# Gate half tiles of an mLSTM stage in four pieces between the products of a chunk, and the first gate tile back in the input projection

## What is computed

```python
def mlstm_chunk(carry, blk):                       # one block of L positions
    C, n, m = carry
    q, k, v, ig, lf = blk
    b = jnp.cumsum(lf, axis=-1)
    dmat = jnp.where(causal, b[..., :, None] - b[..., None, :] + ig[..., None, :], -jnp.inf)
    inter = b + m[..., None]
    m_row = jnp.maximum(inter, dmat.max(-1))
    s = jnp.einsum('bhtd,bhsd->bhts', q, k) * jnp.exp(dmat - m_row[..., None])
    w_prev = jnp.exp(inter - m_row)
    num = w_prev[..., None] * jnp.einsum('bhtd,bhde->bhte', q, C) + jnp.einsum('bhts,bhse->bhte', s, v)
    den = w_prev * jnp.einsum('bhtd,bhd->bht', q, n) + s.sum(-1)
    h = num / jnp.maximum(jnp.abs(den), jnp.exp(-m_row))[..., None]
    ...                                            # C, n and m for the next block

def mlstm_out(h, o, p):
    ...                                            # h is normalised per head
    h = h.reshape(Bsz, S, A_VW) * jax.nn.sigmoid(o.astype(F32))
    return h.astype(o.dtype) @ p['w_pa']
```

## Time and profile before

| | |
|---|---|
| median of 3 runs | 3401.12 us (3394.28 to 3404.74) |
| profiled execution, device time | 3390.82 us |
| its span, first to last instruction | 3389.2 us |
| TensorE busy | 3202.9 us, 95% of the span |
| DVE, ACT busy | 1357.8 us, 1071.0 us |
| mean granted TensorE clock | 0.967 |

### The profile page before, as it was taken

The page is one execution under the profiler, slowest core; times in us unless marked ns, Lnnn a source line. Parts: engine busy times, 40 slices in busy tenths (PEclk is TensorE's granted clock), DMA queues, the critical chain, the costliest instruction groups (busy, mean ns, idle before and its releaser), DMA issues.

```text
span 3389.2 us, 68441 instructions
## 1 busy us (share of the span) xinstructions
PE 3202.9 (95%) x27738; PEld 3007.9 (89%) x27738; DVE 1357.8 (40%) x1874; ACT 1071.0 (32%) x1585; POOL 133.6 (4%) x168
## 2 busy tenths in 40 slices
PE   8999999989998999999999999999899999999997
PEld 7999988867777989999999998988677789899996
DVE  3333345366333453333433334434653334533334
ACT  3222233244343323222232222332534433322223
POOL 0000000000330000000000000000013200000000
PEclk9999999799998999999999999988999989999999
DMA  5232221021552332222233222301035323223321
GB/s 134 87 90 83 82 73 49 7 59 55 204 221 56 87 93 69 87 86 85 60 101 92 86 82 61 95 23 47 23 116 221 147 75 100 62 87 88 88 86 55
DMA packets 443329, 296.56 MB, mean 88 GB/s; under 512 B 24327, under 2 KB 430571, under 8 KB 434985
## 3 DMA queue, kind: packets, MB, share of 16 engines
q1 hardware_dynamic: 430265, 217.05, 22.9%
q0 software_dynamic: 12928, 77.64, 6.1%
HBM read 286.44 MB, written 8.34 MB: 87 GB/s over the span
## 4 chain that ended last, share of the span: by engine, by line
PE 88%; DVE 5%; ACT 3%; issue 2%; DMA 0%; ACTq 0%; DVEq 0%; SPq 0%
PE ps L639 65%; PE ps L998 3%; PE ps L1013 2%; PE ps L747 2%; PE ps L1034 2%; PE ps L679 1%; PE ps L944 1%; DVE x_lo L1605 1%; PE ps L667 1%; PE ps L779 1%; PE ps L1016 1%; PE ps L935 1%; PE ps L922 1%; ACT prob L1418 1%; PE ps L1050 1%
## 5 line engine op out<-in xcount | busy, mean ns | idle before, releaser
L1553 DVE TENSOR_TENSOR w_lo<-w_raw,w_hi 128x1024 fp32r<-128x1024 f32 x436 | 533.5, 1225 | 1006.7 <-ACT w_hi L1198 1001.1
L639 PE MATMUL ps<-x_hi,w_hi 128*128 128x268 f32 x3904 | 814.1, 290 | 25.9 <-DVE x_lo L1605 17.6
L1198 ACT ACTIVATE w_hi<-w_raw 128x1024 fp32r<-128x1024 f32 x436 | 460.1, 1057 | 1170.6 <-PE ps L639 1158.7
L639 PE MATMUL ps<-x_lo,w_hi 128*128 128x268 f32 x3904 | 804.7, 288 | 0.0
L639 PE MATMUL ps<-x_hi,w_lo 128*128 128x268 f32 x3904 | 803.3, 287 | 0.0
L639 PEld LDWEIGHTS ps<-x_hi,w_hi 128*128 128x128 f32 x3904 | 612.9, 190 | 34.1 <-DVE x_lo L1605 24.5
L639 PEld LDWEIGHTS ps<-x_lo,w_hi 128*128 128x128 f32 x3904 | 615.4, 190 | 0.0
L639 PEld LDWEIGHTS ps<-x_hi,w_lo 128*128 128x128 f32 x3904 | 611.9, 189 | 0.0
L639 PE MATMUL ps<-h_hi,w_hi 128*128 128x268 f32 x1408 | 289.8, 288 | 5.0 <-issue 2.9
L639 PE MATMUL ps<-h_hi,w_lo 128*128 128x268 f32 x1408 | 290.9, 288 | 0.0
L639 PE MATMUL ps<-h_lo,w_hi 128*128 128x268 f32 x1408 | 289.4, 287 | 0.0
(11 more groups left out here) (376 smaller groups left out, 3914.1 us busy)
## 6 DMA issues: line engine op xcount, KB each, us to landing
w_raw<-in_ffn_up SPq DMA_DIRECT2D x180, 512.0 KB, 3.8
w_raw<-in_w_in SPq DMA_DIRECT2D x72, 512.0 KB, 3.9
w_raw<-in_ffn_down SPq DMA_DIRECT2D x64, 512.0 KB, 3.8
w_raw<-in_ffn_down SPq DMA_DIRECT2D x32, 384.0 KB, 3.4
w_raw<-in_w_o SPq DMA_DIRECT2D x16, 512.0 KB, 3.8
c_smp<-in_state_C SPq DMA_DIRECT2D x16, 256.0 KB, 3.0
out_new_C_sample<-c_smp SPq DMA_DIRECT2D x16, 256.0 KB, 2.4
w_raw<-in_w_pa SPq DMA_DIRECT2D x16, 256.0 KB, 2.8
```

The lines of the kernel that those rows point to most:

```text
L639: ins = mm(ps[0:m, 2 * p + half, 0:HT], w[:, s, off + t_ * m:off + t_ * m + m], x[part][:, k0 + t_, half * HT:(half + 1) * HT], start=firs ...
L1198: f(w_hi[:, s, :], w_raw[:, s, :], ACT.Copy).then_inc(hi_made, 1)
L1553: v.tensor_tensor(w_lo[:, s, :], w_raw[:, s, :], w_hi[:, s, :].bitcast(F32), ALU.subtract).then_inc(lo_made, 1)
```

## The change

The first gate tile (`B_QK` + 12) becomes the thirteenth tile of the input projection: a whole `product` on TensorE behind the loop, with `hi`, bias and `lo` of block `B_PAIR` + 0 behind it on ACT and DVE. Three tiles are left for the chunk stage, six half tiles: one whole behind `chunk_in(0)`, and one in each of the first five passes, cut into four pieces of 6 matmuls. The pieces stand ahead of `chunk_in(c + 1)`, inside it behind the mask, behind it, and behind line 807. The sixth pass has none. ACT reads each half tile where it did, behind the exponential of its pass. `lo` of `B_PAIR` + 1 to 3 stands behind sample steps 2, 4 and 6 instead of 1, 3, 5 and 7.

```diff
@@ TensorE, mlstm
-                pe.wait_ge(turned_read, l * 9 + 4)
-                gate_part(0, 0, 0, KT)
                 pe.wait_ge(conv_silu, l * 9 + 9)
...
-                def chunk_in(c):
+                def chunk_in(c, gate=None):
...
                     mm(ps[0:CH, 0, 0:HA * CH], ident_b[:, :], mask_b[:, :].unsqueeze(1).to_broadcast([CH, HA, CH]), start=False, stop=True).then_inc(ch_in, 1)
+                    if gate is not None:
+                        gate_part(*gate, 2, 4)
...
                 chunk_in(0)
-                gate_part(0, 1, 0, KT)
+                gate_part(1, 0, 0, KT)
                 for c in range(NCH):
...
                     chunk_we(c, 1)
                     if c + 1 < NCH:
-                        chunk_in(c + 1)
-                    gate_part(1 + c // 2, c % 2, 0, KT // 2)
+                        gate = 1 + (c + 1) // 2, (c + 1) % 2
+                        gate_part(*gate, 0, 2)
+                        chunk_in(c + 1, gate)
+                        gate_part(*gate, 4, 6)
...
-                    gate_part(1 + c // 2, c % 2, KT // 2, KT)
+                    if c + 1 < NCH:
+                        gate_part(*gate, 6, KT)
@@ TensorE, behind the loop of the input projection
+                pe.wait_ge(proj_read, l * PROJ + LINE_TILES)
+                ready(l, B_QK + 3 * HA)
+                product(2, B_QK + 3 * HA, KT, P, XX, True, True).then_inc(w_used, 1)
                 mlstm(l)
@@ ACT, in_projection
-                for t_ in range(3 * HA):
+                for t_ in range(3 * HA + 1):
...
-                conv_out_silu(l, 7)
@@ ACT, mlstm
-                gate_out(0, 0)
                 chunk_act(0)
-                gate_out(0, 1)
+                gate_out(1, 0)
...
-                    gate_out(1 + c // 2, c % 2)
+                    if c + 1 < NCH:
+                        gate_out(1 + (c + 1) // 2, (c + 1) % 2)
...
-                for j in range(4):
+                for j in range(1, 4):
                     hi(l, B_PAIR + j)
@@ DVE, mlstm
-                    if b % 2:
+                    if b in (2, 4, 6):
                         lo(l, B_PAIR + b // 2)
```

More of the change, by code:

```diff
@@ L60 @@
 SLOTS, SLOT_COLS = 4, 1024
-PROJ = 6 + 3 * HA + 2 * HA
+LINE_TILES = 6 + 3 * HA + 1
+PROJ = LINE_TILES + 2 * (HA - 1)
 B_UP1, B_DN1, B_IN, B_QK, B_PAIR, B_MRG, B_WO, B_UP2, B_DN2, B_ALL = 0, 44, 68, 76, 92, 108, 140, 148, 192, 216
@@ L723, in mlstm @@
             def mlstm(l):
-                pe.wait_ge(proj_read, l * PROJ + 18 + 4)
+                pe.wait_ge(proj_read, l * PROJ + LINE_TILES + 4)
                 for c in range(NCH + 1):
@@ L743, in gate_part @@
                             ready(l, k)
-                        pe.wait_ge(proj_read, l * PROJ + 18 + 2 * t_ + half + 4)
+                        pe.wait_ge(proj_read, l * PROJ + LINE_TILES + 2 * (t_ - 1) + half + 4)
                     for kt in range(first, last):
@@ L1280, in in_projection @@
                     bias = prm[:, R_QK + t_:R_QK + t_ + 1]
-                    dst = two(pre[:, t_, 3:3 + TOK]) if t_ < 8 else two(v_fm[:, t_ % 4, :])
+                    dst = two(pre[:, t_, 3:3 + TOK]) if t_ < 8 else two((v_fm if t_ < 12 else og)[:, t_ % 4, :])
                     f(dst, pair((6 + t_) % 4), ACT.Identity, bias=bias).then_inc(proj_read, 1)
@@ L1308, in gate_out @@
                     else:
-                        act.wait_ge(tile_made, KT + l * HA + t_ + 1)
+                        act.wait_ge(tile_made, KT + l * (HA - 1) + t_)
                     f(og[:, t_, half * HT:(half + 1) * HT], ps[:, 3, 0:HT], ACT.Identity,
```

## The result

The changed kernel takes 3440.07 us (median of 6; 3436.17 to 3446.85) against 3400.99 for the kernel before beside it (6; 3394.28 to 3404.74): a ratio of 1.0118 (1.0104 to 1.0132), 39 us slower. The forecast was slower by 17; the direction held, the size did not, and 3440 lies above the range of 3394 to 3434. The profiled executions differ by more, 3437.2 against 3389.2 in span, 48 us.

A forecast was written before the change was run, and what follows sets the result against it. The prediction took the chunk stage to be bound by TensorE's work and its clock. Its terms summed to +8.4 us a layer, +17 in two, which on 3397.7 gave 3415 us; range 3394 to 3434.

The forecast's parts named there:

- Part 1: Tile moved to the projection: first chunk starts 1.3 us earlier but at the low clock; +3.7 us a layer.
- Part 2: Start of passes 1 to 4: first gate matmul waits 0.85 to 0.9 us for its PSUM bank; +2.0 us a layer.
- Part 3: Five passes: the pieces' effect on the clock, 45 us at the low level for 37; +3.7 us a layer.
- rival (a): In the passes, the pieces hold the clock at the full level: -22 us in all, 3376 us; chance 0.08.
- Part 4: Ends of the chunk stage: sixth pass without gate matmuls -0.7, sample steps -0.3 us a layer.

The follow-up runs named there:

- e3: Changed kernel with only the first tile's move kept: half tiles of the passes put back as 12 and 12 matmuls; 3402.89 us, ratio 1.0016.
- e13: Changed kernel with dummies in the gate-bank waits, sixth pass, ahead of the sample steps, and 30 ahead of the first chunk; 3372.67 us, ratio 0.9909.
- e5: Changed kernel with 7 dummy matmuls of 128x256 in the gate-bank wait of passes 1 to 4; 3391.98 us, ratio 0.9975.
- e16: Changed kernel with 16 and 10 dummies in the two waits ahead of the sample steps; 3414.98 us, ratio 1.0046.
- e1: Changed kernel with 12 dummies in each of two waits of the sixth pass; 3431.26 us, ratio 1.0076.
- e4: Kernel before with the half tiles of all six passes in four pieces, first tile left in the chunk stage; 3441.91 us, ratio 1.0128.
- e8: Changed kernel with the first piece joined to the second inside `chunk_in`, removing the gate-bank wait; 3401.86 us, ratio 1.0006.
- e14: Changed kernel with 7 four-row dummies in the gate-bank wait of passes 1 to 4; 3433.74 us, ratio 1.0085.
- e12: Changed kernel with dummies in the gate-bank waits, in the sixth pass and ahead of the sample steps; 3398.20 us, ratio 0.9987.
- e15: Same kernel as e12, run again for a second profiled execution, which took 3397.79 us.
- e9: Changed kernel with 12 and 12 dummies in the sixth pass, 16 and 10 ahead of the sample steps; 3419.42 us, ratio 1.0058.

## Why the prediction was wrong in size

**Part 1** was right. The first chunk began at 572.42 (forecast 572.7), at the low level, and the passes at 583.99 (584.6). e3, which has this part without the pieces, costs -1 to +12 us by its interval.

e13 shows that the low level there came with the wait of 3.8 us ahead of the first chunk: with the wait filled, the stretch from there to the first pass takes 6.9 us at full clock in place of 11.6.

**Part 2** sized the wait's idle time rightly (0.86 us in layer 0's pass 1, 0.85 to 0.9 forecast) and how often it stands wrongly: I had half of the passes start at the low level, without the wait, and all of them start at full clock, so that it stood in the passes 1 to 4 of both layers, some 3.3 us a layer for 2.0. A term that I did not have is the cutting itself: pass 0, without a wait and at clock 1.00, takes 12.02 us where 11.70 was the figure of before, some 2 us a layer with the four others.

**Part 3** foresaw 45 us of low time in the passes. It was 44 in layer 0 and 37.5 in layer 1. Parts 2 and 3 together gave +5.7 a layer, and the passes grew by 8.6 and 5.3. In the sum this was near, partly by luck, since the wait was too small in it and the clock too large. What I did not see is how much hung on the wait. I had named its effect ("the wait of 0.85 fills the gap again") and taken rival (a), that the pieces hold the clock, for unlikely because of it. Without the wait that mechanism is there: the ten passes run at 1.00 (e5), and the total falls to 3392, though not to rival (a)'s 3376: a cut pass with its wait filled takes 12.97 us and not 11.70, and the steps stay low.

**Part 4** is the step that failed, and 30 of the 31 us by which the forecast of +17 missed the 48 of the profiled executions: the sixth pass, the way and the sample steps were put at -1.0 us a layer and measured +15.5 and +12.3, 27.8 in both layers against -2.0. The sum had no clock term there. "The 12 matmuls at the very end stood inside the wait for DVE ...; their going wins nothing" counted time alone, and -0.3 for the steps took it that they would run as before. In its place the runs showed low clock: the sixth pass ends low (PEclk 0.63 and 0.68), the way is low throughout, and the steps are low for 29.5 and 24 us instead of 4.5. e16 puts a price on it: 26 dummies in the two waits took 25 us off.

Why the level came back so late in the steps stays open. The missing 12 matmuls do not explain it alone: e1 has as many dummies in their place and e4 never emptied the sixth pass, and both have steps of 37 us in layer 0, while e3, emptied like the change, has 25. The kernel before entered its steps at the low level as well and was out of it after 4.5 us, in its one profiled execution in both layers. What the runs do show is that the whole loss comes with the pieces (e4, e3), goes with the wait or its filling (e5, e8), and stands as lost clock wherever it stands. The two ways out are not independent parts of a sum: e3 and e8 have a slow layer in the steps and lie within 0.2% of the kernel before all the same, because their passes are shorter than before.

The Trainium skill (TensorE: Matmul & The Clock Gate, section "Why this matters for your kernels") warns of idle gaps between bursts of matmuls. Its warning is of gaps several times as long as the 0.86 us here. I set it aside because fully busy passes were slow. The runs show that gaps far shorter than the page's mattered (e5 and e8, 48 and 38 us), and that being busy did not help where the filling had four rows (e14, 0.59 over 20.77 us).

## What to carry to other kernels

Price a short wait by the granted clock of what follows, not by its length, wherever the stretch already wavers between the levels; the test is cheap, a few 128-row dummies inside the wait. Give every stretch of the sum a clock term, also those that the change hardly touches: here the miss stood in steps whose instructions were the same. One profiled execution shows one outcome of a wavering stretch (3370 and 3398 us for the same kernel, e12 and e15), so take a second before you explain a difference by it. Split wide work into narrow runs only at points where its operands and its bank are free.

## What the runs showed of the hardware

The granted clock in these stretches went with 128-row work and not with busy time: 0.59 over 20.77 us fully busy with narrow filling (e14), 1.00 with the same number of wide dummies (e5). The same instructions can run at two speeds: sample steps of 23.48 us at 1.00 (e9) and 42.01 us at 0.52 (e15), TensorE busy for all but 0.43 us of either. Entered at the full level the steps kept it in eleven layers of eleven; entered at the low one they came out of it after 4 to 40 us, in 23 of 23 within one microsecond behind a run of twelve 128-row dummies. These dummies are half of a step at the low level (2.7 of 5.3 us), and one to eight such runs passed before the clock was back.
